# Squares of two chunks added in f32 by VectorE before the statistics matmuls of a norm

## The reference

```python
def rmsnorm(x, g):
    y = x * rsqrt(mean(x * x, axis=-1) + EPS)
    return y * g

h = rmsnorm(x, norm_ffn1) * (1 + m(1)) + m(0)
x = x + 0.5 * m(2) * swiglu(h, w1, w3, w2)      # swiglu: (silu(h@w1) * (h@w3)) @ w2
h = rmsnorm(x, norm_mix) * (1 + m(4)) + m(3)
x = x + m(5) * mixer(h, ...)
h = rmsnorm(x, norm_ffn2) * (1 + m(7)) + m(6)
x = x + 0.5 * m(8) * swiglu(h, w1b, w3b, w2b)
y = rmsnorm(x, final_norm)
```

## Time and profile before

| | |
|---|---|
| median of 3 runs | 1327.88 us (1327.24 to 1329.37) |
| profiled execution | 1328.26 us |
| its span, slowest core (core 2) | 1326.7 us |
| spans of the 8 cores | 1319.0 to 1326.7 us |
| PE busy | 1249.9 us (94%) |
| DVE busy | 523.0 us (39%) |
| ACT busy | 394.7 us (30%) |
| POOL busy | 183.2 us (14%) |

### The profile page before, as it was taken

One profiled execution on the slowest core, in us unless ns is written; L12 is line 12 of the kernel. 1 busy time (PEld: TensorE's weight loads), 2 busy tenths in 40 slices (PEclk: granted clock), 3 DMA queues, 4 the chain that ended last, 5 costly groups with the idle time before them and its releaser, 6 DMA issues.

```text
span 1326.7 us, 18904 instructions; the slowest of 8 cores (1319.0 to 1326.7 us)
## 1 busy us (share of the span) xinstructions
PE 1249.9 (94%) x6524; PEld 575.5 (43%) x6648; DVE 523.0 (39%) x810; ACT 394.7 (30%) x639; POOL 183.2 (14%) x300
## 2 busy tenths in 40 slices
PE   2679999999999999999999999999999999999996
PEld 1234444444444444344444434444444444444444
DVE  2134234211242344566467656522143121432456
ACT  3265100111001245556544326621100111001344
POOL 3012000100001011121434322310001000000000
PEclk9989999999999999989999989999999999999999
DMA  9982734547726210010412213712313211020113
GB/s 178 222 188 34 125 64 75 86 77 111 114 48 93 68 71 10 1 33 1 96 21 49 93 32 96 127 33 38 59 32 54 43 33 32 1 48 1 64 64 127
DMA packets 34988, 90.95 MB, mean 69 GB/s; under 512 B 4016, under 2 KB 10576, under 8 KB 32720
## 3 DMA queue, kind: packets, MB, share of 16 engines
q0 software_dynamic: 21792, 62.01, 28.5%
q1 hardware_dynamic: 13104, 27.73, 6.1%
HBM read 137.04 MB, written 14.68 MB: 114 GB/s over the span
## 4 chain that ended last, share of the span: by engine, by line
PE 87%; DMA 5%; DVE 2%; issue 2%; ACT 2%; POOL 1%; DVEq 0%; ACTq 0%; POOLq 0%
PE ps L235 87%; DMA sb_arena<-w_ffn 4%; DVE sb_arena L263 1%; ACT sb_arena L248 1%; DMA sb_arena<-w_ada 1%; DVE sb_arena L252 1%; POOL sb_arena L232 1%; ACT L248 0%; POOL sb_arena L259 0%; PE ps L239 0%; POOL sb_arena L252 0%; DVEq L141 0%; ACTq L141 0%; DVEq L1207 0%; POOLq L141 0%
## 5 line engine op out<-in xcount | busy, mean ns | idle before, releaser
L235 PE MATMUL ps<-sb_arena 128*128 128x512 bf16 (+5 forms) x5719 | 1196.5, 366 | 33.2 <-DVE sb_arena L252 5.4
L235 PEld LDWEIGHTS ps<-sb_arena 128*128 128x128 bf16 (+2 forms) x5840 | 539.0, 98 | 681.5 <-issue 72.9
L248 ACT ACTIVATE sb_arena<-ps 128x512 f32<-128x512 f32 (+3 forms) x273 | 161.3, 599 | 707.1 <-PE ps L235 699.0
L252 DVE TENSOR_TENSOR sb_arena<-sb_arena,ps 128x512 bf16<-128x512 f32 (+1 forms) x208 | 143.0, 688 | 480.0 <-PE ps L235 434.2
L263 DVE SCALAR_TENSOR_TENSOR sb_arena<-ps,sb_der,sb_arena 128x512 f32<-128x512 f32 (+1 forms) x200 | 145.2, 729 | 151.8 <-PE ps L235 151.8
L248 ACT ACTIVATE sb_arena<-sb_arena 128x512 bf16<-128x512 f32 (+4 forms) x193 | 122.9, 661 | 82.7 <-DVE sb_arena L263 62.1
L232 POOL DMA_DIRECT2D sb_arena<-w_ffn x88 | 47.2, 546 | 416.5 <-PE ps L235 386.4
L252 DVE TENSOR_TENSOR sb_arena<-sb_arena 128x512 f32<-128x512 f32 x96 | 64.7, 716 | 47.5 <-ACT sb_arena L248 46.9
L259 POOL TENSOR_SCALAR sb_arena<-sb_arena,sb_der,sb_modT 128x512 bf16<-128x512 f32 x44 | 40.8, 928 | 251.0 <-DVE sb_arena L252 242.7
L263 DVE SCALAR_TENSOR_TENSOR sb_arena<-sb_arena,sb_vec 128x512 f32<-128x512 f32 (+1 forms) x72 | 51.6, 736 | 23.0 <-ACT sb_arena L248 19.3
L248 ACT ACTIVATE sb_arena<-sb_arena,sb_modT,sb_der 128x512 bf16<-128x512 f32 x48 | 39.0, 813 | 59.7 <-DVE sb_arena L252 45.4
(11 more groups left out here) (40 smaller groups left out, 165.9 us busy)
## 6 DMA issues: line engine op xcount, KB each, us to landing
sb_arena<-w_ffn POOLq DMA_DIRECT2D x44, 512.0 KB, 8.9
sb_arena<-w_ada POOLq DMA_DIRECT2D x36, 512.0 KB, 9.4
sb_arena<-w_ffn POOLq DMA_DIRECT2D x44, 256.0 KB, 9.3
sb_arena<-x SPq DMA_DIRECT2D x8, 1024.0 KB, 12.9
y<-sb_arena SPq DMA_DIRECT2D x24, 256.0 KB, 2.3
xspill<-sb_arena SPq DMA_DIRECT2D x4, 1024.0 KB, 4.2
sb_arena<-xspill SPq DMA_DIRECT2D x4, 1024.0 KB, 6.6
sb_arena<-w_cv POOLq DMA_DIRECT2D x12, 256.0 KB, 7.2
```

Source lines behind the costliest of these rows:

```text
L235: return P.add("pe", lambda e: e.matmul(out, lhsT, rhs, start=start, stop=stop), reads=flat(reads), writes=flat(writes))
L248: return P.add("act", lambda e: e.activation(out=out, in_=in_, func=func, **kw), reads=flat(reads), writes=flat(writes))
L252: return P.add(eng, lambda e: e.tensor_tensor(out=out, in0=in0, in1=in1, op=op), reads=flat(reads), writes=flat(writes))
```

## The change

`square` writes f32 into one of two places of 2 KB (behind the four places of 1 KB that the sums take), the even chunk into the first, the odd into the second. After each odd one VectorE adds the two in f32 and writes the sum in bf16 into one of four places. `stats` then has four matmuls and not eight. Where the statistics were two pieces of four matmuls, they are one, so the applies of the first FFN move up by one piece.

```diff
--- before.py
+++ after.py
@@ -324,8 +324,15 @@
 
         def square(st, blk, kc):
 
-            st[kc] = P.alloc("sq%d" % kc, SQ + kc * KB, KB)
-            act(bf(SQ + kc * KB, 512), xv(kc, blk), AF.Square, [t_x[kc][blk]], [st[kc]])
+            o = SQ + (4 + 2 * (kc % 2)) * KB
+            t = P.alloc("sqf%d" % (kc % 2), o, 2 * KB)
+            act(f32(o, 512), xv(kc, blk), AF.Square, [t_x[kc][blk]], [t])
+            if kc % 2 == 0:
+                st["even"] = t
+                return
+            i = kc // 2
+            st[i] = P.alloc("sq%d" % i, SQ + i * KB, KB)
+            tt("dve", bf(SQ + i * KB, 512), f32(SQ + 4 * KB, 512), f32(SQ + 6 * KB, 512), ALU.add, [st["even"], t], [st[i]])
 
         def norm_slices(blk, apply, done=None):
 
@@ -340,8 +347,8 @@
 
             def stats(k0, n):
                 for kc in range(k0, k0 + n):
-                    mm(ps[:, 7, :], onesB[:], bf(SQ + kc * KB, 512), kc == 0, kc == 7, [t_ones, st["sq"][kc]], [t_ps[7]])
-                if k0 + n == 8:
+                    mm(ps[:, 7, :], onesB[:], bf(SQ + kc * KB, 512), kc == 0, kc == 3, [t_ones, st["sq"][kc]], [t_ps[7]])
+                if k0 + n == 4:
                     r = f32(RSTD + sl * 2 * KB, 512)
                     st["r"] = P.alloc("rstd%d" % sl, RSTD + sl * 2 * KB, 2 * KB)
                     act(r, ps[:, 7, :], AF.Ln, [t_ps[7]], [st["r"]], scale=1.0 / D, bias=EPS)
@@ -353,9 +360,9 @@
             out = []
             if done is None:
                 out += [(lambda k0=k0: squares(k0, 2)) for k0 in (0, 2, 4, 6)]
-                out += [lambda: stats(0, 4), lambda: stats(4, 4)]
+                out += [lambda: stats(0, 4)]
             else:
-                out += [lambda: stats(0, 8)]
+                out += [lambda: stats(0, 4)]
             out += [(lambda kc=kc: app(kc)) for kc in range(8)]
             return out
```

## The result

The changed kernel takes **1349.24 us** (median of four runs, 1348.84 to 1350.97), the kernel before 1328.62 us beside it (1327.24 to 1330.5). The ratio is 1.0158, with a 95% interval of 1.0145 to 1.017: slower by 20.6 us. The forecast was 1349.

The account below looks back on a forecast made before the run. TensorE, busy 1249.9 of 1326.7 us, was taken as the bound; place terms sum to +16.4 us, the clock adds 4.9, so +21.3 on 1328.26 gives 1349.6, predicted as 1349 us. Range 1342 to 1354, 8 in 10 within 1338 to 1357.

Parts of the forecast that it names:

- Matmuls, 13.0 us: All 15 norms: 60 statistics matmuls removed at 0.216 us of TensorE's queue each, 13.0 us saved where TensorE doesn't then wait.
- Pairs of 2.04 us: Two squares, add and hand-overs become a chain between ScalarE and VectorE: 2.04 us a pair, where two squares took 1.04.
- First FFN, blocks 2 and 3, +2.9 each: TensorE stands until the fourth add is done: +2.9 us instead of -0.9 in each block, +5.7 together.
- First FFN, block 1, -0.9: TensorE waited for the norm's result anyway; the result comes four matmuls earlier: -0.9 us.
- Down units without applies, -0.86 each: Five down-unit stages of both FFNs: the adds just fit, covered by three PSUM banks; -0.86 us each, -4.3 together.
- Third blocks, +1.7 and +2.5: Last stage of each FFN, five applies behind the down units, VectorE already the bound: +1.7 us first FFN, +2.5 second.
- Output projection, block 2, +4.65: The first add stands in VectorE's queue behind the block's last update, so the statistics end late: +4.65 us.
- The blocks behind it, +2.9 each: Output projection, blocks 3 and 0: adds and applies in VectorE's queue lengthen the 15.54 us period by 2.9, twice: +5.8.
- Clock, +4.9: Half-speed stretches behind new stops: +3.4 us in the first FFN, +0.5 three times in the output projection; bounds 0 to +10.
- The adds hide: Rival: adds always finish before TensorE comes, so the 13.0 us come back: 1315 us, faster; chance 0.05.
- The output projection absorbs: Rival: squares there run ahead of VectorE's queue, four norms give 0.9 each instead of costing 11.7: 1333 us; chance 0.10.
- The clock costs more: Rival: half-speed stretches of 6.8 us, also behind stops of 1.5 us: +5 to +9, 1354 to 1358 us; chance 0.20.

Follow-up runs that it names:

- e1_half: Kernel before, with statistics matmuls for the four odd squares alone and no adds (another result): 1316.5 and 1318.1 us, ratio 0.9916.
- e3: Changed kernel with the two squares in bf16 instead of f32, still in the same two places: 1342.46 us, ratio 1.0102.
- e4: As e3, but eight places of 1 KB, one per square, the sum written over the even square: 1328.42 us, ratio 1.0001.
- e6_zeros: Changed kernel with matmuls by zeros filling TensorE's stops at five norms (first FFN blocks 2 and 3, first three of output projection): 1346.35 us, ratio 1.0131.
- e11_stats_early: As e9, with block 1's statistics in the first FFN one up unit earlier, behind the fifth unit: 1319.5 us, ratio 0.9925.
- e5: As e4, but each add recorded behind the next pair's first square, the last one at once: 1320.6 us, ratio 0.9938.
- e9: As e5, with squares of the first FFN's blocks 2 and 3 in pieces of 3, 3 and 2: 1319.5 us, ratio 0.9926.
- e8: As e4, but the adds on GpSimd instead of VectorE: 1323.62 us, ratio 0.9958.

## Why the prediction was right, and where not

The total came out 0.2 us from the median, and part of that is luck: the attention ahead of the output projection gave 1.5 us more than forecast and block 1 1.1 more, while the clock charge was 2 us too high behind the stops and 1.2 us came back at a place that nobody had looked at. The mechanism, two waits that grow out of two places and one queue, is what the traces and the experiments show.

*Matmuls, 13.0 us.* Right: 0.86 a norm by the intervals, some 11 to 12 us by e1_half, where 14 norms were worth 12.1. The Trainium skill (TensorE: Matmul & The Clock Gate, "Back-to-back issue gap") gives some 131 ns, by which four would be worth an estimated 0.52; the runs have 0.86.

*Pairs of 2.04 us.* Measured 2.09: the hand-over from VectorE to ScalarE took 0.15 and not 0.10. The e3, e4 ladder shows that the chain is the largest cause.

*First FFN, blocks 2 and 3, +2.9 each.* Measured +3.1 and +4.4. Of the 4.4, 3.5 stay at full speed: three cores had no half-speed stretch behind block 2's stop, and took 26.7 us for block 3 instead of 23.25, as e6_zeros did. The stop makes 3.0 of that; the other 0.5 is a wait of block 2's own matmuls for an apply on GpSimd, which I had left out (TensorE of core 3):

```profile
106.31 1.67 PE L235 MATMUL ps<-sb_arena 128*128 128x512 bf16 x7
108.29 5.56 PE L235 MATMUL ps<-sb_arena 128*128 128x512 bf16 x25 [0.31 <-POOL sb_arena L259]
```

The prediction also reads its own chain wrongly in one place: it lets three matmuls go at once and charges the clock for one stop of 3.7 us, though by pairs of 2.04 us the third sum is ready only at 114.8. The trace has two stops of 1.72 us with a matmul between. The same holds for its 5.7 us at the output projection.

*First FFN, block 1, -0.9.* The row says +0.2, and still the step held. The statistics took 1.03 us and not 1.89, and TensorE went on 4.54 us behind their end, as before:

```profile
71.53 1.03 PE L235 MATMUL ps<-sb_arena,sb_onesB 128*128 128x512 bf16 x4
77.09 0.59 PE L235 MATMUL ps<-sb_arena 128*128 128x512 bf16 x1 [4.54 <-ACT sb_arena L248]
```

But TensorE came to these statistics 1.0 us later: at 69.1 before and 70.1 after, in the median of the cores, and at 69.9 in e1_half, which has no adds. Ahead of them it waits for weight transfers, 2.0 to 3.3 us at 55 to 57 us before the change, differently on every core. Whether the 1.0 us is theirs alone stays open. e11_stats_early doesn't bear on this: there the statistics stand so early that ScalarE's queue ends last.

*Down units without applies, -0.86 each.* Right at two of five to a hundredth. Two others have the same saving with a clock term on it: the first hides behind +1.1 from half speed after block 3's stop, and the last of the first FFN shows -2.1, since a half-speed stretch that seven cores had at about 535 us before comes on three after. I hadn't counted on gains of that kind. The second FFN's first block shows -0.5; with the late adds of e5 it has the full -0.9, so that 0.4 us there hang on the adds.

*Third blocks, +1.7 and +2.5.* Measured +1.9 and +2.7, and the stop is where the sum put it.

*Output projection, block 2, +4.65.* The chain is as computed, with the first add right behind the update of 808.11: from that update to the end of the statistics it took 7.99 us (to 816.10), where it took 3.19 (802.68 to 805.87), +4.8. The rest of the +6.35, some 1.5 us, lies in the attention ahead, where all cores had a half-speed stretch at 577 to 582 us after and four before; e1_half, which has no adds, has that stretch on all cores too, and its interval is as long as before instead of 0.9 us shorter. *The blocks behind it, +2.9 each:* 3.4, with half speed, and 2.5 without; the first of VectorE's updates came as computed, but two applies behind an add took 1.2 us and not 1.43 (839.71 to the update at 841.52, less 0.60 for the add), so that the block is 0.4 us shorter than computed. *The last, +1.2:* 0.9.

*Start, 0.* Right: the first statistics end 1.6 us later, at 21.0 instead of 19.4, and the waits for the modulation weights take it up.

*Clock, +4.9.* Less, and not as distributed. By the intervals against e6_zeros it is 1.0 and 1.1 us behind the two stops in the first FFN, where 3.4 had been charged, and 0.8 in the output projection's block 3, where 0.5 was; behind the other two stops there nothing can be told. That is 2.9 of 4.9. Elsewhere, some 1.5 came in the attention, behind waits that the change doesn't touch, and 1.2 was given back at about 535 us: 3.2 in all. The total of the half-speed stretches, without the one in which the kernel ends, went from 17.0 to 30.6 us a core to 27.2 to 44.2. The Trainium skill's rule (same page, "HAM oscillation — how this bites in real kernels"), that gaps between bursts throttle the array again, agrees with e6_zeros: filled gaps, clock 1.00.

*The rivals.* "The adds hide" fell in the first FFN; with bf16 squares in eight places and late adds it is true to 2.2 us (e9). "The output projection absorbs" fell by VectorE's queue, and came true for its first norm with eight places (e4). "The clock costs more" fell: it cost some 3 us, not 4.9 plus 5.

## What to carry to other kernels

A matmul saved in front of a wait is worth nothing, and work moved off the bound engine must finish before that engine comes: draw the producers' chain with the durations of the rows, and look at how many buffers it runs through. A pair that shares two places with the next pair turns two engines into one; narrow squares, a place for each and an add recorded behind the next producer turned +20.6 us into some -9. Where an instruction waits in order, what stands behind it counts more than its own duration: a slower add in a queue where no update waits (e8) beat a fast one ahead of the updates (e4).

## What the runs showed of the hardware

- An add of two bf16 squares on VectorE took 425 ns, of two f32 ones 692, for 512 columns; on GpSimd the bf16 one took 1173.
- ScalarE's f32 squares start 0.52 us apart and take 0.63 each, as the bf16 ones did. Hand-overs: 0.15 us from an add on VectorE to ScalarE and to TensorE, 0.10 from ScalarE to VectorE (118.23 to 118.33).
- Half-speed stretches differ between cores that run the same program: 17.0 to 30.6 us in the kernel before, without the one at its end. Two stops of 1.72 us in a row brought one on five cores at one place and on all at the next; a stop of 2.52 us (853.05) on five, one of 2.22 (834.98) on none. They lasted from 3.4 to 13.7 us.
- A change moves such stretches at places it doesn't touch (535 us, the attention at 577 to 582 and 787): some 1 to 2 us each way, more than some terms of the sum.
